# Two expert tables gathered apart, the second summed by 32-column products of four tokens, in one block with the queries

## The reference, cut to what matters

```python
def peer(h, p):                                   # h: tokens x 1024
    n = h.shape[0]
    q = (h @ p['peer_wq']).reshape(n, 8, 2, 128)
    s = einsum('nhcd,chkd->nhck', q, p['peer_keys'])           # 8 heads, 2 halves, 128 keys
    s1, i1 = lax.top_k(s[:, :, 0], 16)
    s2, i2 = lax.top_k(s[:, :, 1], 16)
    cand_s = (s1[..., :, None] + s2[..., None, :]).reshape(n, 8, 256)
    cand_i = (i1[..., :, None] * 128 + i2[..., None, :]).reshape(n, 8, 256)
    top_s, pos = lax.top_k(cand_s, 16)
    eidx = jnp.take_along_axis(cand_i, pos, axis=-1)           # 16 of 16,384 experts a head
    g = jax.nn.softmax(top_s, axis=-1)
    act = jax.nn.gelu(einsum('nd,nhkd->nhk', h, p['peer_u'][eidx]))
    return einsum('nhk,nhkd->nd', g * act, p['peer_v'][eidx])
```

## Time and profile before

| | us |
|---|---|
| median of 3 runs (lowest to highest) | 1579.23 (1577.44 to 1579.65) |
| span of the profiled execution | 1572.5 |
| first gather of experts | at 882.67 |
| last dot | at 1564.58 |
| busy PE, DVE, ACT, POOL | 1312.5, 865.6, 609.3, 432.2 |

### The profile page before, as it was taken

The page is one execution under the profiler, slowest core; times in us unless marked ns, Lnnn a source line. Parts: engine busy times, 40 slices in busy tenths (PEclk is TensorE's granted clock), DMA queues, the critical chain, the costliest instruction groups (busy, mean ns, idle before and its releaser), DMA issues. The chain is left out here.

```text
span 1572.5 us, 18458 instructions
## 1 busy us (share of the span) xinstructions
PE 1312.5 (83%) x5124; PEld 814.4 (52%) x5124; DVE 865.6 (55%) x2312; ACT 609.3 (39%) x1556; POOL 432.2 (27%) x510
## 2 busy tenths in 40 slices
PE   5968999998798997879989677977976788777787
PEld 4846678776697555658878422422322322222222
DVE  1024369996381326761110699799996545544454
ACT  1134238877382304510001244444443444444443
POOL 1331002220121110000000354644688433333331
PEclk9978999999798998889999999999999999999999
DMA  4553223322586540044233599999997999999997
GB/s 157 169 154 106 68 95 121 108 94 81 190 286 238 165 144 1 1 187 178 71 130 130 205 417 402 422 421 422 385 421 283 420 422 422 422 422 422 422 422 324
DMA packets 77068, 391.09 MB, mean 249 GB/s; under 512 B 11385, under 2 KB 22169, under 8 KB 39617
## 3 DMA queue, kind: packets, MB, share of 16 engines
q0 software_dynamic: 43168, 287.34, 44.7%
q1 hardware_dynamic: 33088, 101.32, 18.5%
q10 hardware_dynamic: 736, 1.56, 0.3%
HBM read 378.43 MB, written 11.60 MB: 248 GB/s over the span
## 5 line engine op out<-in xcount | busy, mean ns | idle before, releaser
L1701 PE MATMUL pe_acc<-pe_uv,pe_dg 128*128 128x512 f32 (+1 forms) x1056 | 524.6, 624 | 145.8 <-ACT pe_dg L1747 133.9
L1701 PEld LDWEIGHTS pe_acc<-pe_uv,pe_dg 128*128 128x128 f32 (+1 forms) x1056 | 180.2, 189 | 486.8 <-ACT pe_dg L1747 329.8
L1927 DVE CUSTOM_DVE_ANT_0 pe_uv<-pe_uv,pe_hnat 128x1024 f32<-128x1024 f32 x264 | 321.2, 1218 | 192.8 <-DMA pe_uv<-d_uv,pe_idx 181.0
L1794 POOL DMA_INDIRECT pe_uv<-d_uv,pe_idx x256 | 318.5, 1244 | 337.4 <-PE pe_acc L1701 314.0
L180 PE MATMUL pi_ps<-xn,pi_w 128*128 128x264 f32 x944 | 226.1, 396 | 9.5 <-PEq L86 9.5
L180 PEld LDWEIGHTS pi_ps<-xn,pi_w 128*128 128x128 f32 x944 | 182.0, 196 | 42.1 <-issue 11.3
L1741 ACT ACTIVATE pe_gl<-pe_a 128x1 f32<-128x1 f32 x264 | 53.4, 202 | 348.1 <-DVE pe_a L1927 342.6
L1747 ACT ACTIVATE pe_dg<-cst,pe_w 128x128 f32<-128x128 f32 x256 | 102.8, 401 | 8.3
L1744 ACT ACTIVATE pe_w<-pe_gl,pe_gw 128x1 f32<-128x1 f32 x256 | 75.4, 295 | 32.2 <-ACT pe_gl L1741 1.5
L1776 POOL COPY pe_hrep<-hN 128x128 f32<-128x128 f32 x8 | 2.0, 295 | 301.2 <-POOLq L86 301.2
L1608 PE MATMUL pq_ps<-hN,pq_w 128*128 128x264 f32 x256 | 58.7, 393 | 5.7 <-DMA pq_w<-d_wq 5.7
(11 more groups left out here) (283 smaller groups left out, 1843.4 us busy)
## 6 DMA issues: line engine op xcount, KB each, us to landing
pi_w<-d_w_in SPq DMA_DIRECT2D x71, 512.0 KB, 3.4
mg_w<-d_w_ab SPq DMA_DIRECT2D x8, 1536.0 KB, 6.4
ss_h<-d_state SPq DMA_DIRECT2D x8, 1024.0 KB, 7.3
o_ssm_s<-ss_h SPq DMA_DIRECT2D x8, 1024.0 KB, 8.2
pq_w<-d_wq SPq DMA_DIRECT2D x16, 512.0 KB, 3.4
lg_w<-d_w_in SPq DMA_DIRECT2D x10, 512.0 KB, 6.3
paged<-d_ck POOLq DMA_DIRECT2D x32, 128.0 KB
paged<-d_ck SPq DMA_DIRECT2D x32, 128.0 KB, 4.7
```

Source lines behind the costliest of these rows:

```text
L1701: mm = pe.matmul(acc[0:m, 4 * half:4 * half + 4, :], lhsT, uv[:, r, D_MODEL + half * 512:D_MODEL + (half + 1) * 512], start=False, stop=Fa ...
L1794: pool.indirect_dma_start(uv[:, r, :], None, k.d_uv[:], bass.IndirectOffsetOnAxis(ap=src, axis=0)).then_inc(gathered[r], 16)
L1927: dve.tensor_tensor_reduce(uv[:, r, 0:D_MODEL], uv[:, r, 0:D_MODEL], hnat[:, n, :], 1.0, 0.0, ALU.mult, ALU.add, a[:, r:r + 1]).then_inc(d ...
```

## The change

The two blocks become one, and the rows of `u` and `v` are gathered by gathers of their own from two tables (`d_u`, `d_v`), of 128 rows of 4 KB each.

- The order of the first part: after query columns 0, 2 and 4 PE turns a tile of `h`; after every second column it scores one head of tile 0 (`BANK`, `READ` say in which part of PSUM and after which reading). Tile 0 is chosen in five parts: heads 0, 1, 2 to 3, 4 to 5, 6 to 7.
- `u` is gathered as before, expert i of 128 tokens, to eight slots (`RU`). The dots of a tile fill a 128 x 128 matrix `a`; one gelu (ACT) and one multiplication (DVE, `weigh`) make all weights of the tile.
- `v` is gathered by tokens: PE turns the indices (`turn_indices`), DVE copies them to whole numbers (`copy_indices`), and one gather brings the 128 rows of one token, an expert on each partition, to one of twelve slots (`RV`).
- The sum of a token is then one column: PE turns the weights, and `mask` (four multiplications by a 32 x 32 unit pattern, `eye`) makes for each token a 128 x 32 matrix with its weights in one column and zeros elsewhere. `mix(n, j)` takes four tokens j, 32+j, 64+j, 96+j: for each half of the row one product for each of four groups of 32 columns of PE, which add to 32 partitions of `acc` each.
- The samples: their `h` is spread over the partitions by a product into PSUM (`spread_h`), the dots read it there, their indices and weights are turned by PE; the trip through DRAM is gone.
- The order of the gathers: 128 u of tile 0, 52 v of tile 0 (`AHEAD`), 128 u of tile 1 with the other 76 v of tile 0 between them, 8 u of the samples, 16 v of tile 1, 8 v of the samples, 112 v of tile 1.
- Results leave in halves of 512 columns.

The diff, cut to its core:

```diff
-def peer_queries(nc, k):
+def peer(nc, k):
+    RU, RV, PSB = 8, 12, 2
+    CHOICES = ((0, 0, 1), (0, 1, 2), (0, 2, 4), (0, 4, 6), (0, 6, 8), (1, 0, PH), (2, 0, PH))
+    AHEAD, PAIRS = 52, 120
+    S_AFTER = 4
...
+            for n in range(NT):
+                query(n)
+                if n in (0, 2, 4):
+                    turn_h(n // 2)
+                if n == 2:
+                    pe.wait_ge(k_loaded, 16)
+                if n % 2 == 0 and n:
+                    pe.wait_ge(evacuated, n)
+                    if n // 2 > 4:
+                        pe.wait_ge(s_read, READ[n // 2 - 5])
+                    score(0, (n - 2, n - 1))
...
-                        for half in range(2):
-                            mm = pe.matmul(acc[0:m, 4 * half:4 * half + 4, :], lhsT,
-                                           uv[:, r, D_MODEL + half * 512:D_MODEL + (half + 1) * 512],
-                                           start=False, stop=False, skip_group_check=True)
+            def mix(n, j):
+                nonlocal groups
+                if j % 8 == 0:
+                    pe.wait_ge(masked, 4 * n + j // 8 + 1)
+                for q in range(G4):
+                    pe.wait_ge(v_in[(groups * G4 + q) % RV], 16 * ((groups * G4 + q) // RV + 1))
+                for half in range(2):
+                    for q in range(G4):
+                        mm = pe.matmul(acc[32 * q:32 * q + 32, 4 * half:4 * half + 4, :], wm[:, 32 * q + j, :],
+                                       vv[:, (groups * G4 + q) % RV, half * 512:(half + 1) * 512],
+                                       start=False, stop=False, tile_position=(0, 32 * q), skip_group_check=True)
+                mm.then_inc(accumulated, 1)
+                groups += 1
...
+            turn_indices(0)
+            pe.wait_ge(s_read, FIRST)
+            score(1, range(NT))
+            turn_weights(0)
+            residual(0)
+            for j in range(32):
+                mix(0, j)
+                if j == IDX1_AT:
+                    turn_indices(1)
+                    pe.wait_ge(s_read, FIRST + 1)
+                    score(2, range(NT))
+            turn_weights(1)
...
-                        act.activation(gl[:, r:r + 1], a[:, r:r + 1], ACT.Gelu_apprx_tanh).then_inc(gelued, 1)
-                        act.activation(wt[:, r:r + 1], gl[:, r:r + 1], ACT.Copy, scale=g).then_inc(weighed, 1)
-                            act.activation(dg[:, r, :], k.ident, ACT.Copy, scale=wt[:, r:r + 1]).then_inc(diagonal, 1)
+            def gelu(n):
+                act.wait_ge(dotted, PER * (n + 1) if n < 2 else 2 * PER + TS)
+                    act.activation(wt[:], a[:], ACT.Gelu_apprx_tanh).then_inc(gelued, 1)
...
+            def gather_u(n, i):
+                if nu >= RU:
+                    pool.wait_ge(dotted, nu - RU + 1)
+                src = idx[:, n, i:i + 1] if n < 2 else idxt[:, 2, i:i + 1]
+                pool.indirect_dma_start(u[:, nu % RU, :], None, k.d_u[:], bass.IndirectOffsetOnAxis(
+                    ap=src, axis=0)).then_inc(u_in[nu % RU], 16)
+            def gather_v(n, i):
+                if nv >= RV:
+                    pool.wait_ge(accumulated, nv // G4 - RV // G4 + 1)
+                t = i % G4 * 32 + i // G4 if n < 2 else i
+                pool.indirect_dma_start(vv[:, nv % RV, :], None, k.d_v[:], bass.IndirectOffsetOnAxis(
+                    ap=idxt[:, n, t:t + 1], axis=0)).then_inc(v_in[nv % RV], 16)
+            for i in range(PER):
+                gather_u(0, i)
+            pool.wait_ge(idx_copied, 1)
+            for i in range(AHEAD):
+                gather_v(0, i)
+            for i in range(PER):
+                gather_u(1, i)
+                for j in range(AHEAD, P):
+                    if (j - AHEAD) * PAIRS // (P - AHEAD) == i:
+                        gather_v(0, j)
+            pool.wait_ge(idx_copied, 4)
...
+            def mask(n):
+                    dve.tensor_tensor(wm.rearrange("p (q t) j -> p q t j", q=G4)[:, :, t8, :],
+                                      wq[:, :, t8].unsqueeze(3).broadcast_to([P, G4, 8, 32]),
+                                      eye[:, t8, :].unsqueeze(1).broadcast_to([P, G4, 8, 32]), ALU.mult
...
+            ahead(choose(0), 100)
+            ahead(choose(1), 100)
+            dve.wait_ge(h_read, 1)
+            for c in range(2, FIRST):
+                units = choose(c)
+                for i in range(32 * (c - 2), 32 * (c - 1)):
+                    dot(0, i)
+                    ahead(units, 1)
+                ahead(units, 100)
+            copy_indices(0)
             weights(0)
+            units = choose(FIRST)
+            for i in range(96, PER):
+                dot(0, i)
+                ahead(units, 1)
+            ahead(units, 4)
+            weigh(0)
+            ahead(units, 2)
+            mask(0)
+            ahead(units, 100)
+            weights(1)
...
-        d_uv=A(np.concatenate([npa(peer_u)[0], npa(peer_v)[0]], axis=1)),
+        d_u=A(npa(peer_u)[0]), d_v=A(npa(peer_v)[0]),
+        d_eye=A(np.broadcast_to(np.eye(32, dtype=np.float32), (P, 32, 32))),
```

462 lines of the change are left out of this document (253 added, 209 removed).

## The result

| | before | after |
|---|---|---|
| median, us (lowest to highest) | 1579.44 (1577.44 to 1579.89), 4 runs | 1738.47 (1734.84 to 1740.49), 4 runs |
| span of the profiled execution | 1572.5 | 1733.2 |
| busy PE, DVE, ACT, POOL | 1312.5, 865.6, 609.3, 432.2 | 1030.7, 877.9, 332.0, 709.0 |

The ratio of the times is 1.1007, with a 95% interval from 1.0988 to 1.1025: 10% slower, where 1740 us was forecast. The profiled execution took 1734.84 us. ACT and PE lost some 280 us of work each and POOL gained 277, as the change says; only the last can have made it slower.

What follows compares the result with a forecast made beforehand. The transfer of 264 gathers bounds the kernel (656 of 682 us). First gather 838, then stages ending at 1106, 1158, 1519, 1535 and 1721, span 1733, plus 6.7 for the median: 1740 us; range 1630 to 1835.

Steps and rivals of the forecast that it cites:

- A: First tile's dots, bound by DVE: last dot at 1091 us, first product at 1106.
- B: 40 more v gathers before the first u of tile 1, at 1.29 us each: 52 us, to 1158.
- C: 128 u and 76 v gathers mixed, beside 128 dots and the sample tile's choice; POOL needs 361 us, to 1519.
- D: POOL waits to gather for the samples until tile 1 is weighed, masked and sample indices turned: 16 us, to 1535.
- E: Last 8 u and 136 v gathers, 144 at 1.29 us: 186 us, to 1721.
- I take 0.6 a dot: Hold-up of POOL's gathers by each two-operand SBUF dot: 0.6 us (ends 0 and 1.2), 1.2 beside the sample tile's choice.
- I take 1.29 wherever POOL is undisturbed: Time per gather of 4 KB rows, 1.29 us, from a 410 GB/s stretch; the other end was 1.61 us.
- The signs that I had named: Trace checks: first gather 838, first dot 848, DVE full and DMA share 0.7 in A, 0.7 in C, 1.0 at the end.
- Rival 1: Dots do not hold up POOL, so C takes 263 us and A loses 5: 1637 us; chance 0.15.
- Rival 2: Every dot costs POOL the whole 1.2 us, C + 54 and A + 22: 1816 us; chance 0.18.
- Rival 3: 32-column products run one after another, PE bounds B (+ 27) and E (+ 83): 1850 us; chance 0.14.
- Rival 4: DVE keeps ahead of gathers in A, DMA engines stay full from 838: 1524 us, faster; chance 0.03.

Runs made afterwards that it cites:

- the one-operand run: The changed kernel with all 264 dots replaced by a sum over u alone, one SBUF operand: 1690.52 us, ratio 1.0721.
- the tiny-gather run: The kernel before, 8 KB rows kept, a tiny gather of 16 rows of 64 bytes behind each gather, dots as one-operand sums: 1676.48 us, ratio 1.0627.
- the split alone: The kernel before with each 8 KB row gathered as two 4 KB rows from two tables, all else kept: 1709.37 us, ratio 1.0815.
- the split kernels: The kernel before with 8 KB rows gathered as two 4 KB rows, with two-operand dots (1709.37 us) and with one-operand sums (1687.69 us).
- the run with the other order: The changed kernel with both halves of a token behind each other in the 32-column products, instead of four column groups: 1736.73 us, ratio 1.1006.
- the first half: The kernel before with queries, turning and scoring in the experts' block and early first head, 8 KB rows kept: 1555.59 us; with last choice pieces spread, 1547.53 us.

## Why the prediction was right, and where it was right by luck

| end of stage | predicted | measured |
|---|---|---|
| first gather, first dot | 838, 848 | 836.2, 846.0 |
| A, first product | 1106 | 1109.6 |
| B, first u of tile 1 | 1158 | 1168.9 |
| C, last u of tile 1 (its length) | 1519 (361) | 1490.4 (321.5) |
| D (its length) | 1535 (16) | 1505.6 (15.2) |
| E, last v (its length) | 1721 (186) | 1720 (214) |
| end of the span | 1733 | 1733.2 |

**Start and A** were right in size and cause: last dot of tile 0 at 1092.1 for 1091, DVE busy for 224 of 240 us. Leaving out the dots brought 44 us by the first product, and 56 in all. "Some 75 us of DMA time are given away" was too much: at the rate that these gathers reach, 140 of them need 140 x 1.44 = 202 us, not 181, so some 50 were given away.

**"I take 0.6 a dot"** is the term of C that failed. The hold-up exists; the one-operand run shows 0.36 a dot on POOL, and 25 us of C. I had it from seven gathers with two dots among them, too few to price 128. The stretches of after give it by place: beside the choice (whose own instructions are in it) 125 us for 72 gathers and 90 / 2 = 45 dots, (125 - 72 x 1.24) / 45 = 0.79 instead of 1.2; after the choice POOL is busy 78.34 us for 72 gathers and some 42 dots, (78.34 - 72 x 0.94) / 42 = 0.25 instead of 0.6. The last six pieces of the choice cost 11.5 us where I had put 15: nine gathers in the 22.7 us from 1350.30 to 1372.98, over 9 x 1.24. No gather sat through them all again; the longest takes 6.39 us. C came out 40 us shorter.

**"I take 1.29 wherever POOL is undisturbed"** failed the other way. B ran at 1.43 us a gather, E at 1.49: 7 + 28 us more. The nearest row, 410 GB/s at share 1.01, was one of direct loads, and it told nothing on gathers that follow each other without a pause. The runs put the cause in two places: twice the gathers for the same bytes (the tiny-gather run: 99 of 110 us), which gives 1.445 us a gather in the last hundred of E, 22 of the 28 us; and the wait of 10.29 us behind the samples' products, whose time on PE the prediction put at nothing. (The two overlap by a few microseconds, since the other gathers from 1505 to 1530 run faster, at POOL's 1.24.) The number of slots adds little at twelve, and much at eight (58 us). The other end that I named, 1.61, bounds it.

**Not in the sum either** was DVE's wait of 22.9 us for the turned indices at its dot 16 of tile 1: worth 18.7 us. I had listed what every engine does in C, but not asked where in PE's order the turn stands.

So C was priced 40 too long, although a wait was missing in it, and A, B and E 39 too short. That 1740 met 1738 is a coincidence of these: luck. The verdict, slower, rests on firmer ground: the split alone gives 8%.

**The signs that I had named** say the same. First gather, first dot and a full DVE in A came as said. The DMA share there was to be 0.7 and was 0.88, at 300 GB/s: the bytes moved as forecast (300 / 422 = 0.71), but the engines were busy longer for them. In C it was to be 0.7 and was 0.85, then 0.99; in the last 180 us 1.0, and was 0.94. And "if the v gathers land at another rate than 1.24 to 1.3 us each" came true (1.43, 1.49), so by its own test this part of the prediction was wrong.

**The rivals.** Rival 1 (dots don't hold up POOL, 1637): the one-operand run is that rival made real, and it stands at 1690.5, because 1.29 was too low and the waits for the indices and behind the samples' products were missing. Rival 2 (1.2 a dot, 1816) falls with 0.36. Rival 3 (PE the bound, 1850) falls with 1.93 us a group. Rival 4 fell on A, and would have fallen on the rate of gathers too.

The Trainium skill (SBUF — State Buffer, Who interferes with whom) has a rule by which two SBUF inputs on VectorE contend with a GpSimd instruction that reads SBUF. 1.118 against 0.937 us a gather in the split kernels agree with it, and so do the 0.94 us beside dots with one operand in PSUM; the price is no more than a fraction of a dot. The Trainium skill (TensorEngine Tiling (Array Packing), Key Properties) says that different tiles run in parallel. 1.93 us for eight products agree, and the run with the other order adds that neighbours need not be different tiles.

## What to carry to other kernels

Before splitting a gather, count gathers and not bytes: here twice as many cost some 100 us for the same bytes, with POOL at 1.24 us each and no engine full. Ask of every engine where in its order the work stands that another one waits for: two such places on PE, the turned indices and the samples' products, cost 22.9 and 10.3 us of waiting, and no sum of busy times has them. Test the parts of a change apart: here the first half gained 22 us (29 with the last pieces of a choice spread), and the second lost more than it could save, because the work that it saved, on ACT and PE, lay beside the transfer. A total that fits is no proof of its terms; only stage times and single edits are.
